# Modulation rows spread over two passes, earlier first scores, and later factor products in a two-layer trunk

## The reference

```python
cond = silu(c)
for i in range(2):
    mod = cond @ mod_w[i] + mod_b[i]        # mod_w[i]: 1024 x 6144
    shift1, scale1, gate1, shift2, scale2, gate2 = split(mod, 6)
    h = rms_norm(x, norm1_gain[i]) * (1 + scale1) + shift1
    x = x + gate1 * mixer_i(h)              # swa attention, then gMLP
    h = rms_norm(x, norm2_gain[i]) * (1 + scale2) + shift2
    x = x + gate2 * (square(relu(h @ w1[i])) @ w2[i])

# mixer 0: 16 query heads, 2 key/value heads of 64, windows of 128 keys
q, k = rope(rms_norm(q, q_gain)), rope(rms_norm(k, k_gain))
m = max(max(scores), sink); p = exp(scores - m)
o = (p / (sum(p) + exp(sink - m))) @ v;  y = o @ w_o
```

## Time and profile before

| what | value |
|---|---|
| three timed runs | 2381.03, 2384.39 (median), 2385.55 us |
| the profiled execution's own time | 2383.87 us |
| its span | 2381.7 us |
| TensorE busy | 2278.7 us (96%) |
| VectorE, GpSimd, ScalarE busy | 1282.1, 768.5, 693.0 us |
| DMA | 201.83 MB, mean 85 GB/s |

### The profile page before, as it was taken

One profiled execution on the slowest core, in us unless ns is written; L12 is line 12 of the kernel. 1 busy time (PEld: TensorE's weight loads), 2 busy tenths in 40 slices (PEclk: granted clock), 3 DMA queues, 4 the chain that ended last, 5 costly groups with the idle time before them and its releaser, 6 DMA issues.

```text
span 2381.7 us, 29068 instructions
## 1 busy us (share of the span) xinstructions
PE 2278.7 (96%) x10248; PEld 1819.2 (76%) x10248; DVE 1282.1 (54%) x1570; ACT 693.0 (29%) x938; POOL 768.5 (32%) x568
## 2 busy tenths in 40 slices
PE   2898889999999999999999999999999999999999
PEld 1686567788888888777888888877788888888887
DVE  7877686665665564465334531456755454555321
ACT  2325623332332232233222220223323223322220
POOL 1123330545534643220221222222054454355221
PEclk9998989999999999999999999999999999999999
DMA  6353242222122122223333221222111111111112
GB/s 259 98 159 87 90 172 69 79 89 71 62 82 85 53 84 92 89 89 97 132 132 127 84 87 44 71 71 88 62 45 45 62 53 35 53 62 36 61 44 88
DMA packets 82260, 201.83 MB, mean 85 GB/s; under 512 B 23824, under 2 KB 29840, under 8 KB 81680
## 3 DMA queue, kind: packets, MB, share of 16 engines
q1 hardware_dynamic: 63792, 140.22, 18.1%
q10 hardware_dynamic: 18400, 60.69, 7.2%
HBM read 183.06 MB, written 16.78 MB: 84 GB/s over the span
## 4 chain that ended last, share of the span: by engine, by line
PE 82%; issue 13%; POOL 2%; DVE 2%; ACT 1%; DMA 0%; POOLq 0%; DVEq 0%; ACTq 0%; SPq 0%
PE pp L1420 60%; PE pp L1697 20%; PE pp L1761 1%; POOL pr L420 1%; POOL w_lo L407 1%; PE pp L1735 1%; DVE mod_acc L886 0%; DVE mod_t L964 0%; DMA w_raw<-weights 0%; PE pp L1535 0%; PE pp L1514 0%; ACT tmp L517 0%; DVE mod_late L986 0%; DVE x L956 0%; DVE h_lo L1001 0%
## 5 line engine op out<-in xcount | busy, mean ns | idle before, releaser
L407 POOL TENSOR_TENSOR w_lo<-w_raw,w_hi 128x1024 fp32r<-128x1024 f32 x146 | 357.5, 2449 | 1313.2 <-ACT w_hi L484 1313.2
L1420 PE MATMUL pp<-h_hi,w_hi 128*128 128x512 f32 x1824 | 602.7, 401 | 22.4 <-DVE h_lo L935 7.5
L1420 PE MATMUL pp<-h_lo,w_hi 128*128 128x512 f32 x1824 | 593.6, 396 | 0.0
L1420 PE MATMUL pp<-h_hi,w_lo 128*128 128x512 f32 x1824 | 593.5, 396 | 0.0
L1420 PEld LDWEIGHTS pp<-h_hi,w_hi 128*128 128x128 f32 x1824 | 339.9, 189 | 113.9 <-DVE h_lo L1001 13.1
L1420 PEld LDWEIGHTS pp<-h_hi,w_lo 128*128 128x128 f32 x1824 | 343.8, 188 | 84.4
L1420 PEld LDWEIGHTS pp<-h_lo,w_hi 128*128 128x128 f32 x1824 | 344.1, 189 | 82.5
L1287 DVE SCALAR_TENSOR_TENSOR x<-pp,mod,x 128x512 f32<-128x512 f32 x336 | 252.4, 751 | 241.8 <-PE pp L1697 241.8
L484 ACT ACTIVATE w_hi<-w_raw 128x1024 fp32r<-128x1024 f32 x170 | 179.7, 1057 | 613.5 <-PE pp L1420 502.1
L1697 PE MATMUL pp<-c_hi,w_hi 128*128 128x512 f32 x672 | 265.0, 394 | 0.0
L1697 PE MATMUL pp<-c_lo,w_hi 128*128 128x512 f32 x672 | 265.0, 394 | 0.0
(11 more groups left out here) (161 smaller groups left out, 2270.1 us busy)
## 6 DMA issues: line engine op xcount, KB each, us to landing
w_raw<-weights SPq DMA_DIRECT2D x218, 512.0 KB, 3.5
mod_t<-mod_w ACTq DMA_DIRECT2D x64, 512.0 KB, 4.0
mod_first<-mod_w SPq DMA_DIRECT2D x16, 512.0 KB, 15.5
mod_late<-mod_w ACTq DMA_DIRECT2D x2, 4096.0 KB, 21.3
v_dram<-v_out ACTq DMA_DIRECT2D x16, 512.0 KB, 5.2
vf<-v_dram ACTq DMA_DIRECT2D x16, 512.0 KB, 3.3
x<-x_in SPq DMA_DIRECT2D x4, 1024.0 KB, 8.9
qf<-q_dram SPq DMA_DIRECT2D x32, 128.0 KB, 2.1
```

The lines of the kernel that those rows point to most:

```text
L407: nc.gpsimd.tensor_tensor(out=w_lo[:, s, :, :], in0=w_raw[:, s, :, :], in1=w_hi[:, s, :, :].bitcast(f32), op=ALU.subtract).then_inc(lo_don ...
L1420: last = T.matmul((pp[s] if tile is None else tile)[:, cs], w[:, s, k, :], r[:, k, cs], start=(k == 0 and w is w_hi and r is hi), stop=(k ...
```

## The change

`load_q` gets six slots instead of four (`QSLOTS`), which no longer overlay the rotation's memory, and SyncE fetches the first six before it stores group 2. The scores of steps 0 and 1 are issued on TensorE directly behind the value unit; `mod_columns(3)` moves from slice 2 of the value unit to slice 7 of the unit before; VectorE does `mod_part(3)` and the first sinks before the last group's rotation, and the last factor products after the maxima of step 1. ScalarE loads the exponential's table early, and copies the transposed values between its first exponentials. The second output-projection block (`split_hi` and `split_lo` of unit `U_WO + 1`) is split at the end of attention. The late rows are dealt over both passes: eight in the first, eight in the second, three of these behind its last `low`. `mod_columns(4)` moves to slice 5 of the last unit of the first pass, `mod_part(4)` behind the last `done`, `mod_columns(5)` behind the opening pair, `mod_part(5)` to the end of `closing`, ahead of the MLP's first `even_unit` on VectorE. `late_acc` is gone; one accumulator serves all.

```diff
-LATE_ROWS = ((), (), (0, 1, 2), (3, 4, 5), (6, 7, 8), (9, 10, 11), (12, 13), (14, 15))
+LATE_ROWS = ((0, 0, 1, 2, 1, 2, 2), (0, 0, 1, 0, 1, 1, 2, 0, 3))
+LATE_ORDER = (0, 1, 2, 3, 4, 5, 6, 7, 14, 15, 8, 9, 10, 11, 12, 13)
 # SyncE
-            save_q(2)
             for j in range(2):
                 sp.wait_ge(q_out[j], 16 * 8)
-            sp.wait_ge(q_turned, 4)
-            for t in range(4):
+            for t in range(QSLOTS):
                 load_q(t)
+            save_q(2)
             save_q(3)
 # GpSimd
-            with pool.Fori(0, U_WO // 2 + 1) as pair:
+            with pool.Fori(0, U_WO // 2) as pair:
...
+            split_lo(U_WO // 2, 0)
             # 32 x normalise
+            split_lo(U_WO // 2, 1)
 # ScalarE
+            nc.scalar.activation(root[:, 0:1], root[:, 0:1], ACT.Exp)
             act.wait_ge(gemm, U_V + 1)
             nc.scalar.activation(vt[:, PAD:], pp[1][:, :], ACT.Copy).then_inc(evac[1], 1)
-            split_hi(5, 1)
-            for j in range(4):
+            def values(j):
...
             for t in range(STEPS + 3):
                 if t < STEPS:
                     exps(t)
+                if t < 2:
+                    values(2 * t)
+                    values(2 * t + 1)
...
+                if t == STEPS - 1:
+                    split_hi(U_WO // 2, 1)
 # VectorE, closing, late
                         if u == 2:
                             dve.wait_ge(late_in[0], 16)
-                        if u == 4:
-                            dve.wait_ge(late_in[1], 16)
-                        late_rows(LATE_ROWS[u])
-                        if u == 6:
-                            mod_part(4, zeros=2)
+                        if u < KC - 1:
+                            late_rows(LATE_ROWS[0][u])
+                    mod_part(4)
...
-                    if late and u == 3:
-                        mod_part(5, zeros=0)
+                    if late:
+                        if u == 2:
+                            dve.wait_ge(late_in[1], 16)
+                        late_rows(LATE_ROWS[1][u])
...
                 low(KC - 1, 1, 1)
+                if late:
+                    late_rows(LATE_ROWS[1][KC])
+                    mod_part(5, pp[2])
 # VectorE, query groups (j = 3) and attention
+                if j == 3:
+                    mod_part(3)
                 dve.wait_ge(q_sq, 2 * j + 3)
                 V.tensor_tensor(out=tmp[:, 0, :], ...).then_inc(q_sum, 1)
+                if j == 3:
+                    dve.wait_ge(evac[0], U_WO // 2)
+                    for t in range(2):
+                        sinks(t, 0)
...
                 if t < STEPS:
                     maxima(t)
+                if t == 1:
+                    normed(3)
 # TensorE
-                    unit(pair0 + 3, 0, hi, lo, halves=(0,), hooks={3: columns[0]})
-                    unit(pair0 + 3, 1, hi, lo, halves=(0,))
+                    unit(pair0 + 3, 0, hi, lo, halves=(0,))
+                    unit(pair0 + 3, 1, hi, lo, halves=(0,), hooks={5: columns})
...
-                if columns:
-                    hooks[5] = columns[1]
...
 # TensorE, end of opening_pair
+                if n == 1:
+                    mod_columns(5, mf_used, 4 * KC, tile=pp[2])
...
+                if j == 2:
+                    hooks[7] = lambda: mod_columns(3, mt_used, 2 * KC)
+                unit(2 + j, 0, h_hi, h_lo, hooks=hooks)
...
-                if j == 2:
-                    hooks[2] = lambda: mod_columns(3, mt_used, 2 * KC)
+            scores(0)
+            scores(1)
             head_spread(4)
...
-                if t + 1 < STEPS:
+                if 1 <= t < STEPS - 1:
                     scores(t + 1)
+                if t == 3:
+                    pe.wait_ge(q_cs, 8)
```

More of the change, by code:

```diff
@@ L190, in build @@
         v_tr, v_cp = sem("v_tr"), sem("v_cp")
-        qf_in = [sem(f"qf_in{i}") for i in range(4)]
+        qf_in = [sem(f"qf_in{i}") for i in range(QSLOTS)]
         sc_mm, p_max, p_exp, p_tot = sem("sc_mm"), sem("p_max"), sem("p_exp"), sem("p_tot")
@@ L368, in _ @@
                 load_block(5, s)
-            save_q(2)
             for j in range(2):
                 sp.wait_ge(q_out[j], 16 * 8)
-            sp.wait_ge(q_turned, 4)
-            for t in range(4):
+            for t in range(QSLOTS):
                 load_q(t)
+            save_q(2)
             save_q(3)
-            for t in range(4, NCH):
+            for t in range(QSLOTS, NCH):
                 load_q(t)
@@ L894, in mod_step, with mod_part @@
                 scale_add(mod_t[:, slot, :], k, mt_used)
-            def mod_part(part, tile=None, zeros=1):
+            def mod_part(part, tile=None):
                 dve.wait_ge(mod_mm, part + 1)
-                if zeros:
-                    V.memset(mod_acc[:, :], 0.0).then_inc(acc_zero, zeros)
-                    dve.wait_ge(acc_zero, part + (zeros - 1))
+                V.memset(mod_acc[:, :], 0.0).then_inc(acc_zero, 1)
+                dve.wait_ge(acc_zero, part)
                 V.tensor_reduce(out=col_sum[:, :], in_=(pp[3] if tile is None else tile)[:, :].rearrange("p (k c) -> p k c", c=P),
@@ L976, in done, with late_rows @@
                     add_half(i, s, half)
-                def late_rows(rows):
-                    for q in rows:
+                def late_rows(count):
+                    for _ in range(count):
+                        q = late_count[0]
+                        row = LATE_ORDER[q]
                         dve.wait_ge(mf_used, q + 2 * KC)
[L981 to L987, removed]
+                        scale_add(mod_late[:, row, :], row % KC, mf_used)
+                        late_count[0] += 1
                 def scaled(k, s, half):
@@ L1134, in sinks, with normed @@
                               ).then_inc(sinks_in, 1)
+            def normed(j):
+                dve.wait_ge(q_turned, j + 1)
+                dve.wait_ge(q_bc, j + 2)
+                for part in (oa, ob):
+                    V.tensor_tensor(out=part[:, 1 - j % 2, :], in0=part[:, 1 - j % 2, :], in1=pp[2][:, :],
+                                    op=ALU.mult).then_inc(q_cs, 1)
             for j in range(4):
@@ L1155, in _ @@
                     mod_part(2)
[L1156 to L1160, removed]
                 if j < 3:
                     mods(2)
[L1163 to L1166, removed]
                 if j < 3:
+                    normed(j)
                     mods(2)
@@ L1569, in head_spread @@
                 spread(q_bc)
[L1571 to L1578, removed]
-                if j == 2:
-                    hooks[2] = lambda: mod_columns(3, mt_used, 2 * KC)
-                unit(2 + j, 1, h_hi, h_lo, hooks=hooks)
-            head_spread(4)
             def scores(t):
-                pe.wait_ge(qf_in[t % 4], (t // 4) * 16 + 16)
+                pe.wait_ge(qf_in[t % QSLOTS], (t // QSLOTS) * 16 + 16)
                 if t >= 2:
                     pe.wait_ge(p_exp, t - 1)
+                if t == 0:
+                    pe.wait_ge(kf_in, 16 * 4)
+                    pe.wait_ge(pads, 1)
                 if t in (0, 1, NCH, NCH + 1):
@@ L1593, in scores @@
                         rows = slice(HD * g, HD * g + HD)
-                        last = T.matmul(score_tile(t)[:, g, r, 0:P], qf[rows, t % 4, P * r:P * r + P], kf[rows, keys],
+                        last = T.matmul(score_tile(t)[:, g, r, 0:P], qf[rows, t % QSLOTS, P * r:P * r + P], kf[rows, keys],
                                         start=True, stop=True)
                 last.then_inc(sc_mm, 1)
+            normed_pair(0)
+            unit(1, 0, h_hi, h_lo, hooks={3: lambda: head_squares(0)})
+            unit(1, 1, h_hi, h_lo, hooks={1: lambda: head_spread(0), 4: lambda: head_squares(1)})
+            for j in range(3):
+                hooks = {2: lambda: head_spread(j + 1)}
+                if j == 2:
+                    hooks[7] = lambda: mod_columns(3, mt_used, 2 * KC)
+                unit(2 + j, 0, h_hi, h_lo, hooks=hooks)
+                hooks = {4: lambda: head_squares(j + 2)}
+                if j == 0:
+                    hooks[2] = lambda: mod_columns(2, mt_used, KC)
+                unit(2 + j, 1, h_hi, h_lo, hooks=hooks)
+            scores(0)
+            scores(1)
+            head_spread(4)
             def turn(t):
@@ L1617, in mix @@
                 last.then_inc(pv_mm, 1)
-            pe.wait_ge(kf_in, 16 * 4)
+            pe.wait_ge(evac[1], U_V // 2 + 1)
             pe.wait_ge(d_lo, 1)
-            pe.wait_ge(pads, 1)
-            scores(0)
-            pe.wait_ge(evac[1], U_V // 2 + 1)
             for j in range(4):
@@ L1653, in _ @@
             pe.wait_ge(p_cp[0], STEPS // 2)
-            closing(U_WO // 2, h_hi, h_lo, 1, begun=True,
-                    columns=(lambda: mod_columns(4, mf_used, 3 * KC), lambda: mod_columns(5, mf_used, 4 * KC, late_acc)))
+            closing(U_WO // 2, h_hi, h_lo, 1, begun=True, columns=lambda: mod_columns(4, mf_used, 3 * KC))
```

17 lines of the change are left out of this document (10 added, 7 removed).

## The result

The changed kernel takes 2369.9 us (median of 5, 2366.4 to 2372.8) against 2381.0 for the kernel before: ratio 0.9946, 95% interval 0.9934 to 0.9958. It is faster by about 13 us. The forecast was 2369.4.

A forecast was written before the change was run, and what follows sets the result against it. TensorE, busy 96% of the span, was the bound, so only its gaps and slow clock could be won. -7.5 - 10.7 - 0.8 + 4.5 = -14.5 from 2383.87 gave 2369.4 us; own range 2366 to 2373, overall 2363.5 to 2377.

The forecast's parts named there:

- A: Start of attention: first normalisation earlier, loop keeps its rate; 7.5 us won, bounds 5 to 9.5.
- The chain: Start of attention: instruction times followed from value unit through scores, maxima and products to first normalisation at 202.2, 7.5 earlier.
- only as a bound: Start of attention: lower bound of 5 us won, if loads 6 and later, behind group 3's stores, come late.
- my three signs that the forecast is wrong: Second pass: TensorE waits for VectorE's weight splits; clock stays at 0.50 through several units; attention loop steps wait for `qf`.
- the upper bound: Start of attention: 9.5 us won if the clock stays up in the loop's first steps.
- three things removed: Start of attention: the wait, the table load and a ScalarE weight split of 1.05, all counted within the 7.5 us.
- B: Output projection, first pass: 3.9 us lost in place of 16.1, less 1.5 for the clock; 10.7 won, bounds 6 to 13.
- C: Output projection, second pass: `mod_columns(5)` leaves it, 0.8 us won; up to 2 cost if VectorE's backlog stays.
- rival that the first pass stays bound: Output projection, first pass: VectorE stays the bound through GpSimd's splits, 6.5 us given back, 2376 us; chance 0.14.
- The 1.5 for the clock: Output projection, first pass: cost of a lower clock after the 2.9 us idle stretch, from 0 to 2.7.
- rival without a clock cost: Both new gaps leave the clock up and attention starts at full clock: 1.5 + 1.5 and 2 more won, 2364.5; chance 0.13.
- D: Entry of the MLP: unit starts 3.0 us later behind late rows and `mod_part(5)`, plus 1.5 clock; costs 4.5, bounds 1.5 to 6.

The follow-up runs named there:

- the experiment on part 4's transposes: Changed kernel with part 4's transposes at slice 3 of the second pass's first unit, one slice ahead of the row sums; ratio 0.9924 to the kernel before.
- all three edits: Changed kernel with first even_unit before mod_part(5), part 4's transposes one slice before the row sums, query loads 6 and 7 before group 3's stores; 2359.5 and 2360.8 us.

## Why the prediction was right

**A, start of attention, 7.5 forecast, 8.0 in the profile and 5.1 with these edits alone.** The chain was right almost instruction by instruction: head sum 189.15 (189.4), first normalisation 201.81 (202.2), SyncE's late loads 206.29 (some 5 us behind 201.4). What I had only as a bound was real: the query of step 6 is waited for. That the loop's steps would wait for `qf` was one of my three signs that the forecast is wrong; one step does, for 2.1, and the forecast survived it because the full clock in the first steps, which I had only as the upper bound, came as well. I had put the loop's rate down as unchanged, and its total is (72.9 us for 31 steps, as before), but by two things that cancel. Before, the first four steps ran at a low clock and took 8.4 us:

```profile
208.00:214.00 6.00, 4.79 (x32) 3.45 (x32) 4.07 (x8) 3.37 (x14) 2.08 (x2) 0.63 0.64 158
```

Now they run at full clock and take 6.9, 1.5 less; the two steps behind them, with the wait for the query, take 7.6 instead of 5.9, 1.7 more. And my "three things removed" were not three: in the new order nothing is later without the early table load. That the wait for the sinks, and the exponentials late behind it, carried the gain is argued from the chain; no run takes the early sinks or the early scores away alone, so how the 8 us divide among them is not shown.

**B and C, the two passes, 10.7 + 0.8 forecast, 11.7 measured.** Waits of 3.0 and 0.7 against 2.9 and 0.8 forecast. VectorE, blocked by GpSimd in every unit, was late for part 4 at the place named and, by 0.7, for the row sums, and nowhere else, and the second pass took its rows without a wait on TensorE. The rival that the first pass stays bound did not come; the experiment on part 4's transposes shows that one such wait was left, worth 5.4 in this trace together with the 0.7 and the clock, and 4 to 6 over all traces. The 1.5 for the clock was a mean of two outcomes that both occur: nearly nothing in three traces, 1 to 2 in four. So the rival without a clock cost was right for this gap in three executions of seven.

**D, entry of the MLP, 4.5 forecast, 5.5 measured.** The product ends 9.0 us behind the last `low` in the trace (8.7 forecast). TensorE's start moves by 3.3 relative to the second reciprocal (3.0 forecast), and the clock behind the wait costs 2.2, where I had taken 1.5 out of 0 to 2.7. In the profiled execution the clock fell behind both new waits, as the rule of the Trainium skill that I had cited (TensorE: Matmul & The Clock Gate, "The HAM clock gate") has it; but by it I had the sum 2.4 us slower, 5.4 for the two stretches. They cost 1.7 (the 5.4 of the experiment less 3.7 of waits) and 2.2: 3.9, between my 3.0 and that. The wait of 4.1 at the entry was followed by 0.50 to 0.59 over the next 3 us in all seven traces that have it; the wait of 3.0 was not followed by a lower clock in three of seven, and there the rule, as I applied it, does not hold; the measurement decides.

The sum, -14.5, stands against -14.6 in the times of the profiled pair and -14.2 in their spans. A won 0.5 more than forecast and D cost 1.0 more. In the timed medians the difference is 11.1, or 14.5 if the 2384.4 of the first three runs is taken for the kernel before, which read 2381.0 beside the changed kernel. An agreement of 0.5 us (2369.4 against 2369.9) is luck where executions of one kernel differ by 6; that in the profiled pair the terms come out within 1 us each, with the releasers that were named, is not.

## What to carry to other kernels

- Work that is moved off one wait is paid for where it lands: three rows and a reduction moved behind the last `low` cost 5.5 us there (4.8 to 5.8 over seven traces), because one small product that frees a tile was queued behind them. Look at each landing place for the first instruction that another engine needs, and put it first.
- Place a dependent step by where its producer is done: the same transposes six slices later waited for nothing, and TensorE had matmuls to do in between.
- Before expected gains are added up, take each from the stretch that the edit touches, not from the timed difference of the kernels.
- When a prefetch is made deeper, count what stands in the same queue between the last prefetched item and the next one.

## What the runs showed of the hardware

A wait of 2 us on TensorE in a sparse stretch was followed by a granted clock of 1.00 in one execution and 0.77 in another, of nearly the same program, and so cost 0 or about 1 us on top. In dense stretches, read over the 3 us behind the wait: waits of 1.1 (four traces) and of 1.5 to 1.7 (the kernel before and the attention edits alone, twice each) were followed by 1.00, one of 2.2 in the latter two by 0.75 and 0.72. The same wait of 3.0 to 3.2 was followed by 1.00 in three traces and by 0.50 to 0.67 in four; a wait of 4.1 by 0.50 to 0.59 in all seven. An eight-element add on VectorE took 2.30 us beside a weight split on GpSimd and 0.17 without one (L913, at 185.72 and 332.99). The exponential's table load took 1.28 us, with the next instruction of ScalarE 0.01 behind it. Two executions of the same program (all three edits) differed by 4.5 us before the first edited instruction, with a clock of 0.84 instead of 1.00 in the first 60 us; differences of 2 us need the marks of a trace, not times alone.
